# When GpSimd's scatters are released in the pair stage of a FoX/GLA/PEER block

## What is computed

```python
scores = einsum('thpc,hpnc->thpn', q, sub_keys)          # 8 heads, 2 x 128 keys
s_top, i_top = top_k(scores, 16)
best, pos = top_k(all sums of a first and a second key, 16)
expert_idx = ...                                          # 128 experts of 16384 for each token
gates = softmax(best)
act = gelu(einsum('td,tkd->tk', h, expert_u[expert_idx]))
out = einsum('tk,tkd->td', act * gates, expert_v[expert_idx])
```

## Time and profile before

| | us |
|---|---|
| median of 3 runs | 1817.13 |
| the three runs | 1816.70, 1817.13, 1829.67 |
| the profiled execution | 1816.11 |
| its span, first to last instruction | 1814.4 |

### The profile page before, as it was taken

One profiled execution on the slowest core, in us unless ns is written; L12 is line 12 of the kernel. 1 busy time (PEld: TensorE's weight loads), 2 busy tenths in 40 slices (PEclk: granted clock), 3 DMA queues, 4 the chain that ended last, 5 costly groups with the idle time before them and its releaser, 6 DMA issues.

```text
span 1814.4 us, 25731 instructions
## 1 busy us (share of the span) xinstructions
PE 1782.6 (98%) x9402; PEld 1511.6 (83%) x9402; DVE 1257.8 (69%) x2436; ACT 739.1 (41%) x1225; POOL 1033.9 (57%) x771
## 2 busy tenths in 40 slices
PE   9999999999999999999989999999999999999998
PEld 6777778887888888888889999998888888888886
DVE  6334261112588999898857777773599989988886
ACT  5734463222243323333445655553443333333331
POOL 6432414343253467787776677665588887777410
PEclk9999999999999999999989999999999999999999
DMA  5764643235132344444434544446899999999971
GB/s 195 253 211 147 185 129 98 88 104 186 59 105 82 117 151 136 149 143 147 130 111 141 162 154 160 150 140 208 317 374 382 392 390 388 391 372 371 370 271 70
DMA packets 189967, 368.69 MB, mean 203 GB/s; under 512 B 27905, under 2 KB 109953, under 8 KB 189714
## 3 DMA queue, kind: packets, MB, share of 16 engines
q1 hardware_dynamic: 101216, 209.74, 34.3%
q10 hardware_dynamic: 53810, 89.90, 13.9%
q0 software_dynamic: 34816, 67.41, 10.1%
HBM read 305.96 MB, written 61.01 MB: 202 GB/s over the span
## 4 chain that ended last, share of the span: by engine, by line
PE 93%; DMA 2%; ACT 2%; DVE 1%; issue 1%; another core or an unknown queue 1%; POOL 0%; ACTq 0%; SPq 0%; DVEq 0%
PE bank L578 24%; PE bank L582 24%; PE bank L581 24%; PE bank L958 18%; DMA x<-in_x 1%; PE bank L870 1%; PE bank L741 1%; PE bank L714 1%; PE bank L727 1%; PE bank L787 0%; DMA gates<-gate_scratch 0%; DMA xT_raw<-in_xT 0%; PE bank L796 0%; DMA stage<-in_mix_stream 0%
## 5 line engine op out<-in xcount | busy, mean ns | idle before, releaser
L536 POOL DMA_INDIRECT gate_scratch<-scat_gate,scat_idx x384 | 445.8, 1161 | 180.8 <-issue 97.0
L486 POOL TENSOR_TENSOR w_lo<-stage,w_hi 128x1024 fp32r<-128x1024 f32 (+1 forms) x105 | 248.5, 2387 | 374.7 <-ACT w_hi L1044 338.5
L1044 ACT ACTIVATE w_hi<-stage 128x1024 fp32r<-128x1024 f32 (+1 forms) x284 | 292.4, 1042 | 175.8 <-PE bank L582 148.7
L578 PE MATMUL bank<-x_hi,w_lo 128*128 128x512 f32 (+1 forms) x864 | 336.6, 390 | 0.8 <-issue 0.6
L582 PE MATMUL bank<-x_hi,w_hi 128*128 128x512 f32 (+1 forms) x864 | 334.5, 387 | 0.0
L581 PE MATMUL bank<-x_lo,w_hi 128*128 128x512 f32 (+1 forms) x864 | 334.5, 387 | 0.0
L578 PE MATMUL bank<-w_hi,wt_lo 128*128 128x512 f32 x768 | 298.9, 389 | 0.4 <-DVE wt_lo L1936 0.4
L582 PE MATMUL bank<-w_hi,wt_hi 128*128 128x512 f32 x768 | 298.8, 389 | 0.0
L581 PE MATMUL bank<-w_lo,wt_hi 128*128 128x512 f32 x768 | 298.8, 389 | 0.0
L1677 DVE TENSOR_TENSOR w_lo<-stage,w_hi 128x1024 fp32r<-128x1024 f32 x178 | 216.9, 1221 | 72.0 <-ACT w_hi L1044 49.5
L523 POOL DMA_INDIRECT gat<-in_expert_v,eidx x128 | 154.0, 1203 | 112.1 <-DVE bank L1661 63.5
(11 more groups left out here) (289 smaller groups left out, 3130.8 us busy)
## 6 DMA issues: line engine op xcount, KB each, us to landing
stage<-in_expert_uT SPq DMA_DIRECT2D x128, 512.0 KB
stage<-in_expert_v SPq DMA_DIRECT2D x128, 512.0 KB
stage<-in_mix_stream SPq DMA_DIRECT2D x84, 512.0 KB
gate_scratch<-zeros SPq DMA_DIRECT2D x32, 768.0 KB, 7.4
act<-activation_scratch ACTq DMA_DIRECT2D x32, 768.0 KB
gates<-gate_scratch ACTq DMA_DIRECT2D x32, 768.0 KB
activation_scratch<-act_out_a ACTq DMA_DIRECT2D x64, 256.0 KB
activation_scratch<-act_out_b ACTq DMA_DIRECT2D x64, 256.0 KB
```

The costliest lines, as they stand in the source:

```text
L486: nc.gpsimd.tensor_tensor(w_lo[:, slot, 0:width], stage[:, slot % STAGE, 0:width], w_hi[:, slot, 0:width], ALU.subtract).then_inc(split_do ...
L536: nc.gpsimd.indirect_dma_start(out=gate_cells, out_offset=bass.IndirectOffsetOnAxis(ap=scat_idx[:, b, k:k + 1], axis=0), in_=scat_gate[:, ...
L578: ins = mm(dst, l_lo, r_hi, start=first, stop=False)
L1044: act_f(w_hi[:, slot, 0:width], stage[:, slot % STAGE, 0:width], ACT.Copy).then_inc(hi_done, 1)
```

## The change

One line: the rounding of `product_due` is moved. Before, cell 155 + c waits for floor(c x 224 / 216) + 1 products, after for 7 x floor(c x 32 / 216) + 1. So the cells of a pair, six or seven of them, all wait for the same product, the one numbered 7q + 1 in `PRODUCTS`, and not each for one of its own.

```diff
@@ -88,7 +88,7 @@
 
 def product_due(cell):
 
-    return (cell - EARLY_CELLS) * 7 * PAIRS // PAIR_CELLS + 1
+    return (cell - EARLY_CELLS) * PAIRS // PAIR_CELLS * 7 + 1
 
 
 def cycle(q):
```

## The result

Over 20 runs each on one chip the changed kernel takes 1824.18 us in the median and the kernel before 1815.16 us. The ratio of the comparison is 1.0057 with a 95% interval of 1.0039 to 1.0074: slower by some 9 us, about half a per cent. The forecast was 1817.0 us and no change. The range (1804 to 1830) holds the time; the claim that nothing moves is wrong.

A forecast was written before the change was run, and what follows sets the result against it. PE was taken as the bound, GpSimd's time as worth nothing by itself. All terms were 0, so 1816.1 us of the profiled execution stayed; with the median of runs at 1817.1, the forecast was 1817.0 us, range 1804 to 1830.

The forecast's parts named there:

- What bounds the kernel: Whole kernel: PE bounds it, busy 98% of 1814.4 us; in the pairs PE loses 24 us, mostly in two stretches.
- Moved on GpSimd: GpSimd in the pairs: same scatter density, small waits become about one of 1 to 2 us a pair; term 0.
- Rival B: In the pairs, PE's pauses last as long as GpSimd runs on: slower, 1834.6 us; chance 0.12.
- The lengthening of the first stretch by 4.5 us: Start of the pairs: cells 164 to 168 no longer wait, GpSimd pauses 6.3 us later, costing PE 4.5 us.
- one more bad stretch of 12.1 us: In the pairs: one added stretch of PE pauses, 12.1 us, counted in the slower price of 1834.6 us.
- The argument against B: Before 905.3 GpSimd scatters without pause while PE keeps pace, 120 matmuls in 14.5 us, so long runs needn't stall PE.
- The second argument: End of the first bad stretch: the only instruction-queue packet, 0.02 MB, between 918.5 and 920 points at PE's own instruction supply.
- Rival C: In the pairs, PE's pauses go away: 16.7 us faster, 1800.4 us, or 1805 with the first alone gone; chance 0.09.
- Rival D: In the pairs, DVE becomes the bound by losing over 3.1 us a pair: slower, 1846 us; chance 0.05.
- DMA: Scatter packets in the pairs get 10% denser, landings under 0.1 us a pair later; term 0, bound 3 us.
- who waits for GpSimd: In the pairs nobody; the last scatter ends 12.8 us before the first gates load; gain 0.
- The signs named: In the pairs: GpSimd's waits for PE fall from 59 to about 32, near 50 us total; last scatter ends 1258 to 1264.

The follow-up runs named there:

- compute: Kernel before with each of the pairs' 216 scatters replaced by three GpSimd multiplications in its own memory, no DMA: 1952.77 us, 1.0695, on a chip with pauses.
- none: Kernel before with the pairs' 216 scatters left out: 1.0005 and 0.9996 on chips without pauses; as eight copies 1911.52 us against 1948.92.
- free: Kernel before with the 216 scatters waiting for no product: 1.0004 and 1.0003 on chips without pauses, 2085.69 us, 1.1453, on one with.
- half: Kernel before with cells waiting in groups of three or four, two a pair: 1.0005 on a chip without pauses, 1.0008 on one with.
- double: Kernel before with cells waiting in groups of thirteen or fourteen, one for two pairs: 1.0008 and 1.0000 without pauses, 1947.50 us, 1.0691, with.
- e7: Kernel before run as eight equal copies, one on each core, instead of a single copy: 1948.92 us; the single copy took 1815.08 us.
- e9: Eight copies of kernel before with the 216 scatters of the pairs left out: 1911.52 us against 1948.92 us for eight copies of before.
- e12: The changed kernel again, against kernel before (1786.20 us) on a chip without pauses: 1.0000.
- e14: All 216 scatters issued without a wait for a product, against kernel before (1786.20 us) on a chip without pauses: 1.0003.
- e17: Kernel before with scatter counts 145, 226, 13 instead of 155, 216, 13, giving ten backlog cells products of their own: 1818.69 us, 1.0017.

## Why the prediction was wrong, and where it was right

**What bounds the kernel** held: PE is the bound, and the pairs have 24 us of lost time which are no semaphore's. The reading that "GpSimd's time is worth nothing by itself; the question is only what it does to PE" was right as well, and so was the place that it pointed to.

**The step that failed** is the term *Moved on GpSimd*, costed at 0: "the stream keeps the same density; many small waits become about one of 1 to 2 us for each pair". It measured 8.6 us in the pairs of the profiled execution and 9.0 us between the medians. The waits were priced as the loss of an idle engine. They are also what cuts the scatters into runs and what stops them when PE stands. The density did stay the same in after (226 or so scatters in the pairs, 241.5 us busy against 247.6); how they were bunched did not. The same 216 scatters gave 1.0057, 1.0691 and 1.1453 as the groups grew to 7, 14 and all of them. The average of a stream was taken for its shape.

**Rival B had the mechanism** and was given 0.12. Its price, 17.6 us over the forecast, was worked out from one chain of events and was twice the 9.0 us measured. Its parts came out differently. The lengthening of the first stretch by 4.5 us didn't happen: cell 162 met the threshold of product 8 while only seven were done, so GpSimd stopped at 909.7 and the stretch lost 5.0 us instead of 12.1. That is luck and not the change: before asks product 8 of this cell too, but in after's execution the pairs began 3.9 us later while GpSimd was about 5 us ahead (cell 155 at 900.7 and not 905.8). The "one more bad stretch of 12.1 us" was several short ones instead. The argument against B, "GpSimd scatters without pause elsewhere while PE keeps its pace (120 matmuls in 14.5 us before 905.3)", is right as a fact and weak as an argument. GpSimd had run unbroken since 837.3 by then, for 68 us, but with one scatter every 1.70 us up to 889.9 and one every 1.43 us in the pairs. So it shows that an unbroken run alone isn't enough, and not that runs are harmless. The second argument, the packet on the instruction queue where the first stretch ended, fell too: in the stretches of after at 903.3 to 911.3 and 1175 to 1180.4 that queue moved nothing and PE still came free (in the third, 1236 to 1242.4, it moved one packet).

**Rival C** (the pauses go away) happened in no run of after on a chip that has them, and in the three comparisons without pauses neither kernel has one. Its price, 16.7 us, was too low as a bound: on a chip without pauses the pairs are 27 us shorter and the whole kernel 30 us (1815 against 1785). **Rival D** (DVE becomes the bound) is refuted for this change by 688 ns and 31.3 us; that DVE can hold PE up is shown by `compute` (7.7 us in 27 waits). **DMA** and **who waits for GpSimd** held: a scatter stayed at 1.07 us; the last one moved from 1260.8 to 1269.7 with PE itself, outside the 1258 to 1264 named, and the first gates load from 1274.5 to 1286.9, so the cover is 1286.9 - 1270.6 = 16.3 us, more than the 12.8 before.

**The signs named** came in part: DVE's first wait for the gates stayed (10.0 us, 9.6 after), and GpSimd's waits for PE were to fall from 59 to at most 32 and came to 44 of 65.0 us in total. The count misleads, in before as well: 17 of the 44 (and 20 of the 59) are mere 0.3 us of issue that a product happened to end in. Of the 32 groups 23 waited over 0.5 us before their first scatter. And "more stretches with PE on issue (B)" was the one that came.

**Shown** are: the pauses need GpSimd's indirect DMAs (`none` on eight cores, and the second half of `free`) and not only a busy GpSimd (`compute`); their cost grows with what GpSimd may issue while PE stands, with nothing else changed (half, after, double, free: 1.0008, 1.0057, 1.0691, 1.1453; each against before on the same chip, double and free on one, half on another, after in the first comparison; how much of the step from after to double is the chip's isn't known); they end when the scatters stop; some chips or dies have none. **Open** is whether a run's length or its pace decides, and what inside the chip an indirect DMA of GpSimd takes from PE. Bandwidth, DVE and ACT are ruled out by the rows of `free`; how PE's instructions or its semaphores are served isn't seen in a trace, beyond the steps of 0.70 us. Open too is what makes one die differ from another. A single comparison can't tell: the single copy of before ran at 1785 to 1786 us in three comparisons and at 1815 to 1823 in the others, and the chip's number alone doesn't settle it, since the comparisons of `e7` to `e9` and of `e12` to `e14` bear the same number with 1815.1 and 1786.2 us; whether that was another machine, or the other die of the same chip, isn't known. A threshold near 8 us of unbroken scatters fits after and `double` and no more: before, after and `half` all have longer runs without a pause, and before and `e17` have single pauses after four scatters (1235.8 in before). Half and after were not run side by side on a chip with pauses.

## What to carry to other kernels

A wait on an engine that is off the critical path isn't free to remove or to coarsen: ask what it throttles, and how the work behind it will run on when the engine that it waits for stalls. Where the bound engine shows pauses with no semaphore to blame, lay the start and end of each beside the runs of the others in time, with the pace of each run, and not beside an average over the stage, and raise the suspected dose until it shows; keep streams of indirect DMAs in short runs, tied one by one to the progress of the engine that matters (in threes or fours was not told from this, and not shown to be as good). Try a change of this kind on more than one chip, since a chip that doesn't have the effect says "no change" with a very tight interval.

## What the runs showed of the hardware

- An unbroken stream of GpSimd's indirect scatters (128 values of 4 bytes each, one every 1.26 us) can bring PE from 0.121 us a matmul to 304.1 / 122 = 2.5 us, for as long as it goes on (`free`), with the clock at 0.50, that is 1.2 GHz. The clock falls after the pauses have begun, as in before, and is back at 2.4 GHz only some microseconds after they end (in after the last pause ends at 1180.33 and the clock is 1.00 again in 1186 to 1188).
- It begins 7.4 to 10.9 us into a run in nine places of eleven in after, and 7.4 to 8.7 us in where `double`'s scatters came every 1.27 to 1.30 us; at one every 1.45 us or slower, runs of 17 to 20 us passed without a pause over 0.45 us. A long pause ends 1 to 2 us after the run, but 21 us after a run of 216.
- In the worst of it PE starts single matmuls at whole multiples of 0.70 us, mostly 2.80 us (`free`).
- GpSimd's indirect gathers do it too: 17.6 us of waits on "issue" on core 3 of `none` with eight copies, behind the pairs.
- It isn't there on every chip. Where it is absent, the kernel before takes 1785 us and not 1815, and 216 unthrottled scatters beside PE cost nothing (1.0004 and 1.0003). With eight copies only cores 0 to 3 had it.
- The Trainium skill, "Runtime: NRT & Kernel Launch", Instruction fetch mechanics, has the fetch of an engine's instructions as mostly hidden. On the chips without pauses the trace agrees (2716 matmuls in 331.0 us with no wait on "issue"). On the others something holds back PE's issue that this page doesn't tell of, and no run here shows that it is the fetch.
